# Memory attention of an encoder layer: transposes, probability scaling and expert choices queued in another order

## What is computed

```python
def memory_cross_attention(hn, memn, w_q, w_kv, w_o):
    q = (hn @ w_q).reshape(bsz, t, XA_HEADS, XA_HEAD_DIM)
    k, v = jnp.split(memn @ w_kv, 2, axis=-1)
    ...
    p = jax.nn.softmax(s, axis=-1).astype(v.dtype)
    o = jnp.einsum('bhtm,bmhd->bthd', p, v).reshape(bsz, t, D_XA)
    return o @ w_o

def hierarchical_moe(hn, w_rg, w_re, w_gate, w_up, w_down):
    g_prob = jax.nn.softmax((xf @ w_rg), axis=-1)
    g_top, g_idx = lax.top_k(g_prob, 1)
    ...
    e_top, e_idx = lax.top_k(jax.nn.softmax(e_sel, axis=-1), TOP_K_IN_GROUP)
    e_top = e_top / jnp.sum(e_top, axis=-1, keepdims=True)
    weights = g_top * e_top
    ...
```

## Time and profile before

| | us |
|---|---|
| median of 3 runs | 1222.16 (1222.14 to 1222.35) |
| profiled execution, time | 1222.25 |
| its span, first to last instruction | 1220.4 |
| TensorE busy | 1145.5 (94%) |
| VectorE busy | 642.2 (53%) |
| ScalarE busy | 469.8 (38%) |
| GpSimd busy | 233.0 (19%) |

### The profile page before, as it was taken

How to read it: one execution, slowest core, us unless ns; L and a number is a source line. 1 busy time by engine, 2 the same in 40 slices (tenths; PEclk the granted TensorE clock), 3 DMA queues, 4 the chain that set the end, 5 groups by cost and what they waited for, 6 DMA issues and landing times.

```text
span 1220.4 us, 18992 instructions
## 1 busy us (share of the span) xinstructions
PE 1145.5 (94%) x6854; PEld 916.9 (75%) x6854; DVE 642.2 (53%) x1244; ACT 469.8 (38%) x982; POOL 233.0 (19%) x337
## 2 busy tenths in 40 slices
PE   6999999999997999999999999999995999999956
PEld 5888888878884666888898788778784788887732
DVE  6332333212115897333465663754467998885256
ACT  6322333211005786111332433544323666674223
POOL 3322322200000000100100000100013333554344
PEclk9999999999997999999999999999996999999979
DMA  9573552834139424522221001912797999989967
GB/s 319 131 263 104 160 163 80 308 82 99 38 78 227 123 57 130 206 93 69 85 75 70 1 1 69 313 72 98 279 344 265 346 372 344 371 300 350 407 261 274
DMA packets 108427, 226.58 MB, mean 186 GB/s; under 512 B 28854, under 2 KB 48318, under 8 KB 108222
## 3 DMA queue, kind: packets, MB, share of 16 engines
q1 hardware_dynamic: 83822, 167.86, 40.6%
q0 software_dynamic: 17856, 43.02, 10.6%
q10 hardware_dynamic: 6672, 14.69, 3.8%
HBM read 180.89 MB, written 69.78 MB: 205 GB/s over the span
## 4 chain that ended last, share of the span: by engine, by line
PE 85%; DVE 4%; DMA 3%; issue 3%; ACT 2%; SPq 2%; POOL 1%; ACTq 0%; DVEq 0%; POOLq 0%
PE bank L570 18%; PE bank L572 18%; PE bank L571 18%; PE bank L2291 6%; PE bank L2219 3%; PE bank L2257 3%; PE bank L2089 3%; PE bank L2075 2%; PE bank L2064 2%; PE bank L2228 2%; PE bank L2153 1%; PE bank L2277 1%; DMA at<-v_att 1%; DVE at L565 1%; PE bank L1934 1%
## 5 line engine op out<-in xcount | busy, mean ns | idle before, releaser
L570 PE MATMUL bank<-at,at 128*128 128x512 f32 (+1 forms) x1192 | 442.4, 371 | 5.7 <-DVE at L565 2.5
L572 PE MATMUL bank<-at,at 128*128 128x512 f32 (+1 forms) x1192 | 432.1, 363 | 0.0
L571 PE MATMUL bank<-at,at 128*128 128x512 f32 (+1 forms) x1192 | 431.4, 362 | 0.0
L570 PEld LDWEIGHTS bank<-at,at 128*128 128x128 f32 x1192 | 226.4, 190 | 41.3 <-DVE at L565 3.3
L572 PEld LDWEIGHTS bank<-at,at 128*128 128x128 f32 x1192 | 225.9, 190 | 35.2
L571 PEld LDWEIGHTS bank<-at,at 128*128 128x128 f32 x1192 | 226.5, 190 | 32.5
L565 DVE TENSOR_TENSOR at<-at,at 128x1024 fp32r<-128x1024 f32 (+2 forms) x162 | 180.6, 1128 | 92.7 <-ACT at L560 90.2
L560 ACT ACTIVATE at<-at 128x1024 fp32r<-128x1024 f32 (+2 forms) x162 | 154.5, 988 | 163.4 <-DVE at L1510 51.4
L894 POOL TENSOR_TENSOR at<-at 128x1 f32<-128x1 f32 x88 | 23.7, 269 | 560.2 <-ACT at L1250 283.8
L2291 PE MATMUL bank<-at,at 128*128 128x512 f32 x156 | 74.2, 597 | 3.3 <-ACT at L1324 3.0
L990 POOL DMA_INDIRECT y_tok<-at,at x39 | 39.4, 1010 | 133.4 <-DVE at L1860 98.4
(11 more groups left out here) (213 smaller groups left out, 1351.0 us busy)
## 6 DMA issues: line engine op xcount, KB each, us to landing
at<-in_w_exp_gate SPq DMA_DIRECT2D x39, 512.0 KB
at<-in_w_exp_up SPq DMA_DIRECT2D x39, 512.0 KB
at<-in_w_exp_down SPq DMA_DIRECT2D x39, 512.0 KB
at<-y_tok SPq DMA_DIRECT2D x24, 512.0 KB, 9.7
at<-in_w_in SPq DMA_DIRECT2D x6, 1024.0 KB, 11.4
xT_hi_all<-at POOLq DMA_DIRECT2D x12, 512.0 KB, 3.9
xT_lo_all<-at POOLq DMA_DIRECT2D x12, 512.0 KB, 5.7
at<-xT_hi_all SPq DMA_DIRECT2D x3, 2048.0 KB, 10.3
```

Of the source, the lines that this page charges most:

```text
L570: nc.tensor.matmul(out, w_hi, x_hi, start=(k == 0), stop=False)
L571: nc.tensor.matmul(out, w_lo, x_hi, start=False, stop=False)
L572: last = nc.tensor.matmul(out, w_hi, x_lo, start=False, stop=(k == len(terms) - 1))
```

## The change

Four edits, of order alone; the instructions are the same.

1. The turn of `h` tile 3 (with its eviction, splits, the normalisation of tile 4 and the mean square of tile 5) stands behind `v_mem` 0 instead of behind `v_mem` 3.
2. With the sixth `PT` of a chunk (n % 8 = 5) all `px` up to the eighth are put in the list, instead of each ahead of its own `PT`.
3. Behind the last `o` group the turns of `moe` tiles 4 and 5 come ahead of `xo 8 0`; the router groups 4 to 6 and the turns of tiles 6 and 7 follow one place sooner among the `xo` groups, and parts 2 and 3 of `choose(0)` hang on `route 5` and `xo 9 0`.
4. For the last group of tiles the two subtractions for the gates leave `choose(2)` and come as `last_gate_differences` behind it, ahead of `keep_experts(1)`.

```diff
@@ -361,7 +361,9 @@
         interleave([(mm, "k_mem", h, seq) for seq in range(2) for h in range(XH)], [(T_of, "h", n) for n in range(3)])
-        interleave([(mm, "v_mem", n) for n in range(4)], [(T_of, "h", 3)])
+        mm("v_mem", 0), T_of("h", 3)
+        for n in range(1, 4):
+            mm("v_mem", n)
@@ -393,8 +395,8 @@
-        out_group(8, 0), route_T(4), out_group(8, 1), route_T(5), route_group(4)
-        out_group(9, 0), route_T(6), route_group(5), out_group(9, 1), route_T(7), route_group(6)
+        route_T(4), route_T(5), out_group(8, 0), route_group(4), out_group(8, 1), route_T(6), route_group(5)
+        out_group(9, 0), route_T(7), out_group(9, 1), route_group(6)
         count_stage(0)
         out_group(10, 0), route_group(7), out_group(10, 1), route_T(8)
@@ -423,7 +425,7 @@
-        choose_after = {("mm", "xo", 8, 0): (0, 0), ("mm", "xo", 8, 1): (0, 1), ("mm", "xo", 9, 0): (0, 2), ("mm", "route", 5): (0, 3),
+        choose_after = {("mm", "xo", 8, 0): (0, 0), ("mm", "xo", 8, 1): (0, 1), ("mm", "route", 5): (0, 2), ("mm", "xo", 9, 0): (0, 3),
@@ -444,8 +446,9 @@
             if st[0] == "PT":
-                order += [("px", n) for n in range(scaled, st[1] + 1)]
-                scaled = max(scaled, st[1] + 1)
+                past = st[1] // 8 * 8 + 8 if st[1] % 8 >= 5 else st[1] + 1
+                order += [("px", n) for n in range(scaled, past)]
+                scaled = max(scaled, past)
@@ -1612,7 +1615,8 @@
-                    step(nc.vector.tensor_tensor(lg, lg, over_tokens(g_max, NG), ALU.subtract))
+                    if g < 2:
+                        step(nc.vector.tensor_tensor(lg, lg, over_tokens(g_max, NG), ALU.subtract))
@@ -1623,9 +1627,8 @@
-                    diff = nc.vector.tensor_tensor(logit[:, tiles, NG], e_max2, e_max, ALU.subtract)
-                    if g == 2:
-                        diff.then_inc(route_exp, 1)
+                    if g < 2:
+                        nc.vector.tensor_tensor(logit[:, tiles, NG], e_max2, e_max, ALU.subtract)
@@ -1637,6 +1640,12 @@
+            def last_gate_differences():
+                tiles = slice(TG * 2, TG * 3)
+                lg = logit[:, tiles, 0:NG]
+                step(nc.vector.tensor_tensor(lg, lg, over_tokens(g_max, NG), ALU.subtract))
+                nc.vector.tensor_tensor(logit[:, tiles, NG], e_max2, e_max, ALU.subtract).then_inc(route_exp, 1)
@@ -1666,6 +1675,7 @@
                     if n == 2:
+                        last_gate_differences()
                         keep_experts(1)
                     place_tokens(n)
```

## The result

The changed kernel took 1214.93 us (median of 6 runs) against 1222.15 us before, a ratio of 0.9944 (95% interval 0.9933 to 0.9954): 0.56% faster, 6.8 us. The profiled execution took 1215.29 us, its span 1213.3 us. One run of the kernel before, at 1323.84 us and a granted clock of 0.837, is left out of every figure here. The forecast was 1214.6 us.

A forecast was written before the change was run, and what follows sets the result against it. Six TensorE waits in memory attention were taken as what the change can remove; the expert stage is TensorE's own work. 4.24 + 2.1 + 0.90 + 0.29 = 7.53 us off 1222.16 gave 1214.6 us, range 1212.3 to 1218.5.

The forecast's parts named there:

- the likeliest case: The forecast itself: 1214.6 us, own range 1213.6 to 1215.6, chance 0.68.
- the sum: Savings of the four parts in memory attention added up: 4.24 + 2.1 + 0.90 + 0.29 = 7.53 us.
- Part 1: Around h tile 4 and q 0 0: idle and half rate both go, 4.24 us, bounds 2.77 and 4.24.
- the rival of the clock: Clock falls a few router groups sooner, ahead of group 10, or returns later: 1216.1 to 1217.6 us; chance 0.12.
- Clock still falls: Lower bound of part 1 at tile 4: 2.77 us, without the 1.47 us of half rate.
- Part 2: Probability tiles scaled earlier: 0, 0.60 and 1.5 us in the three chunks, 2.1 us, bounds 0.6 and 3.0.
- Part 3: Router tiles 4 and 5 fill the wait before xo 8 0: 0.90 us, VectorE limiting; bounds 0 and 1.6.
- the 1.6 that was named as the sign: Sign of being right: TensorE's wait for the residual sum (line 1701) about 1.6 us in place of 0.7.
- Part 4: Two subtractions leave the last choice of experts: 0.29 us off the 5.1 us wait, bounds 0 and 0.4.
- a wait of 4.8 us: Sign of being right: TensorE's wait for the last choice of experts (line 1635) at 4.8 us, from 5.1.
- VectorE did not hand part 3 back: Rival: VectorE's reordered queue delays the chain to xo 10 0; part 3 and 0.6 of part 2 go, 1216.1 us; 0.08.
- the scatters: Rival: in the expert stage result scatters fall behind the two result buffers, making it slower, up to 1231 us; chance 0.04.

The follow-up runs named there:

- both_moved: Changed kernel with probability scaling ahead of a chunk's fifth transpose instead of its sixth, and the first count behind xo 10 0; ratio 0.9924 to before, 1211.7 us.
- count_behind_sum: Changed kernel with the first count, and VectorE's token placing after it, moved one group later, behind xo 10 0; ratio 0.9943 to before.
- px_alone: Kernel before with only the scaling of probabilities put ahead of the sixth transpose of eight; ratio 0.9993.
- h3_alone: Kernel before with only the turn of h tile 3 moved behind v_mem 0; ratio 0.9972.
- gate_alone: Kernel before with only the two subtractions for the gates taken out of the last choice; ratio 0.9999.
- without_router_turns: Changed kernel with the earlier turns of router tiles 4 and 5 undone; ratio 0.9966 to before.

## Why the prediction was right, and where its terms were off

**The direction, the order of the terms and the time held.** 1214.6 us was forecast, 1214.93 measured, inside the likeliest case's own range. Between the two profiles the stage from v_mem 0 to the first gather shrank by 8.4 us (272.99 to 264.62), the sum had 7.5; the span shrank by 7.1, because in the profile after v_mem 0 began 0.9 us later, in code that the change does not touch, and the first experts took 0.3 longer. That the time came within 0.3 us of the forecast is in part luck. With the 2.7 us that part 1 gives against the other four profiles of the old order, the same sum ends at 1216.2 us, next to the price of the rival of the clock (1216.1) and outside the likeliest case's range; beyond the 0.6 us of a later fall of the clock at the choice, the runs do not show what made up for the difference.

**Part 1** (4.24 forecast): 4.1 between the two profiles, and the idle went as described.

```profile
676.16 1.04 PE L2163 MATMUL bank<-at,at 128*128 128x128 f32 x8
676.96 0.47 PE L573 MATMUL bank<-at,at 128*128 128x512 f32 x1
...
682.53 1.03 PE L2163 MATMUL bank<-at,at 128*128 128x128 f32 x8
```

In this timeline of TensorE after, tile 4's turn is followed at once by q 0 0, and tile 5's comes 6.37 us later (11.38 - 3.08 = 8.30 before, from 677.41). The term was mis-sized all the same as a forecast of the median: its 1.47 us of half rate was read as a fixed part of the old order, and four of five profiles of that order don't have it. The lower bound, 2.77, is the typical worth. "Clock still falls" was the wrong name for that bound: it is the case in which it had not fallen before.

**Part 2** (2.1): 2.25 us, in the thirds forecast (0, 0.6, 1.7). Taking PT out of VectorE's queue in thought, and asking only what VectorE has in between, gave each third.

```profile
796.84 0.16 DVE L1737 RECIPROCAL at<-at 128x2 f32<-128x2 f32 x1
797.03 0.69 DVE L1740 TENSOR_TENSOR at<-at,at 128x512 f32<-128x512 f32 x1
797.64 0.68 DVE L1711 TENSOR_TENSOR at<-at,bank 128x512 f32<-128x512 f32 x1
```

VectorE's timeline after: scaling first, then the residual sum, the order of the earlier trace rows turned round.

**Part 3** (0.90): 1.02 us up to xo 10 1, by the chain that was named. After, VectorE runs

```profile
878.97 1.28 DVE L1689 SCALAR_TENSOR_TENSOR at<-at,at,at 128x1024 f32<-128x1024 f32 x1 [0.97 <-POOL at L899]
880.17 0.42 DVE L1655 TENSOR_TENSOR at<-at,bank 128x256 f32<-128x256 f32 x1
...
883.53 0.69 DVE L1711 TENSOR_TENSOR at<-at,bank 128x512 f32<-128x512 f32 x1
```

with 0.97 us of idle in place of 2.11, router group 6 evicted ahead of the normalisation, and 3.36 us from placing to the residual sum, as in the earlier trace rows; TensorE waits 1.5 us, near the 1.6 that was named as the sign. The step that failed is the one not made: a lengthened wait was priced at its own length, and not at what the clock may do behind it.

**Part 4** (0.29): 0.28 to 0.34. The sign given for it, a wait of 4.8 us, was wrong for the changed kernel (5.6): a wait is counted from the end of the work ahead of it, and slots 1 ended sooner there at full clock (2.8 us behind the start of router group 11, 4.3 before).

**The clock**, a rival with 0.12, mattered more than it was given. It fell in other places than the one named: not ahead of router group 10, but behind the wait at xo 10 1 (two of nine profiles that have that wait at 0.7 us or more; none of the three without it), and, in the changed kernel's favour, later at the choice, worth 0.6 us. The Trainium skill ("TensorE: Matmul & The Clock Gate", HAM oscillation) blames idle gaps of TensorE for such falls, but longer ones than these. Here a fall came behind 2.0, 0.8 and 1.5 us of idle (at tile 4 and twice at xo 10 1), and at 910.5 us in the profile of before behind none; and the same gap is followed by a fall in one execution and by none in the next. That last fits what the Trainium skill states in Part 1 of the same page, that the gate does not restart with the kernel; no run here shows the gate's own phase.

**The other rivals fell.** VectorE did not hand part 3 back beyond the share in the sum. No time was lost to the scatters, but they were misread: the prediction has one wait of ScalarE for a scatter, and the profile of before has five, of 1.5 to 3.7 us; the one of 2.2 us is not the longest. The profile after has two:

```profile
1026.80 0.60 ACT L1332 ACTIVATE at<-bank 128x512 f32<-128x512 f32 x1 [1.93 <-DMA y_tok<-at,at]
1114.13 0.60 ACT L1332 ACTIVATE at<-bank 128x512 f32<-128x512 f32 x1 [3.25 <-DMA y_tok<-at,at]
```

So the loads of weights did not push the scatters back: the waits are fewer than before, and from the first down product to the end every kernel took 276.2 to 276.5 us. Why the repeated ratio is 0.9963 and the first 0.9944 is left open. The changed kernel's medians agree (1214.93 and 1215.19 us), those of the kernel before do not (1222.15 and 1220.42); the intervals overlap, and the sum with part 1 at 2.7 (6.0 us, 0.9951) lies between.

## What to carry to other kernels

Move a step in the queue of the engine that does it: strike from the list what that engine has no work for, and see whether anything is left between the old place and the new; here that made one third of an edit worth nothing and pointed to a better order. Where a saving ends in a wait for another engine's queue, look for what stands in that queue ahead of the awaited result and could stand behind it (here 1.6 us for one exchanged line). A half-rate stretch in one profile is not a term of the sum until other profiles of the same order show it too.

## What was not expected of the hardware

The same code ahead of the change differed by up to 3.8 us between profiled executions: v_mem 0 began between 651.26 and 655.05 us. The clock is part of it again. Behind a wait of 1.8 us (before) or 2.1 us (both_moved) near 267 us it fell in one and not in the other:

```profile
266.00:272.00 6.00, 4.19 (x12) 3.05 (x11) 3.11 (x3) 1.83 (x2) 0.00 (x0) 0.74 0.31 64
```

```profile
266.00:272.00 6.00, 3.92 (x17) 2.93 (x17) 3.11 (x3) 2.04 (x2) 0.00 (x0) 1.00 0.32 67
```

The first row is before (clock 0.74, 12 matmuls begun), the second both_moved (1.00, 17 begun, although it waited longer). It fell in eight of the twelve profiles; in those four without, v_mem 0 began at 651.26 to 652.35 us, in the eight with it at 652.43 to 655.05. It is not all: before and count_behind_sum have this fall and the next one (from 371 or 372 to 385 us) alike, and their v_mem 0 began 2.6 us apart; what that is stays open. Behind a wait of 0.8 us at xo 10 1 the clock fell in px_alone, and in h3_alone, gate_alone and without_router_turns it did not. At tile 4 and at xo 10 1 a fall cost 1.4 to 1.6 us, more than some of the waits that it followed.
